# Last decode round of a hybrid-mixer kernel: where two branch granules and one row scaling stand in each engine's order

## The reference

```
u = rms_norm(x) @ w_in                      # HGRN2 q/f/i/gate, differential-attention q/k/v, merge gates
o_hg = hgrn2_recurrence(...)                # chunkwise, per head, with a state
o_hg = rms_norm(o_hg) * silu(hgate)
y_hg = o_hg @ w_branch_hg
p    = softmax(q k^T * s + bias)            # two maps per head, over prompt or over pages
o_da = rms_norm((p[0] - lam * p[1]) @ v) * 0.8
y_da = o_da @ w_branch_da
mixed = (sigmoid(g_hg) * y_hg + sigmoid(g_da) * y_da) @ w_out
x = x + rms_norm(mixed);  x = x + rms_norm(ffn(rms_norm(x)))
```

## Time and profile before

| | before |
|---|---|
| median of three runs | 1906.81 us |
| profiled execution, its time | 1907.26 us |
| profiled execution, span of the trace | 1905.7 us |
| PE busy | 1894.5 us (99% of the span) |
| DVE busy / ACT busy | 1044.4 us (55%) / 829.0 us (44%) |
| granted PE clock | 0.999 of full speed |
| last round and the first eight branch granules | about 780 to 838 us of the span |

### The profile page before, as it was taken

How to read it: one execution, slowest core, us unless ns; L and a number is a source line. 1 busy time by engine, 2 the same in 40 slices (tenths; PEclk the granted TensorE clock), 3 DMA queues, 4 the chain that set the end, 5 groups by cost and what they waited for, 6 DMA issues and landing times.

```text
span 1905.7 us, 38358 instructions
## 1 busy us (share of the span) xinstructions
PE 1894.5 (99%) x14806; PEld 1784.0 (94%) x14806; DVE 1044.4 (55%) x1342; ACT 829.0 (44%) x1099; POOL 74.5 (4%) x119
## 2 busy tenths in 40 slices
PE   9999999999999999999999999999999999999998
PEld 9999888888888888799999999999999999999998
DVE  7443655646555465665547844445444455545555
ACT  6333454535444354554445433333333334445454
POOL 1001010000000000000000000000000000000000
PEclk9999999999999999999999999999999999999999
DMA  8877898989999899988444544544444544544541
GB/s 310 179 259 256 320 351 335 376 323 354 349 339 364 321 364 352 320 309 287 153 157 146 174 158 145 172 167 163 161 153 157 167 165 156 164 160 147 177 155 56
DMA packets 123982, 444.13 MB, mean 233 GB/s; under 512 B 14581, under 2 KB 18709, under 8 KB 123856
## 3 DMA queue, kind: packets, MB, share of 16 engines
q1 hardware_dynamic: 112720, 402.31, 58.8%
q0 software_dynamic: 9968, 39.48, 7.0%
q10 hardware_dynamic: 1232, 1.47, 0.2%
HBM read 423.28 MB, written 22.54 MB: 234 GB/s over the span
## 4 chain that ended last, share of the span: by engine, by line
PE 97%; DVE 1%; DMA 1%; ACT 1%; issue 0%; SPq 0%; ACTq 0%; DVEq 0%
PE ps L426 23%; PE ps L428 22%; PE ps L427 22%; PE ps L1838 5%; PE ps L1839 5%; PE ps L1840 5%; PE ps L928 3%; PE ps L963 3%; PE ps L1480 3%; PE ps L437 1%; PE ps L937 1%; DMA raw<-w_hg 0%; PE ps L749 0%; PE ps L736 0%; DVE ffn L1800 0%
## 5 line engine op out<-in xcount | busy, mean ns | idle before, releaser
L369 DVE TENSOR_TENSOR w_lo<-raw,w_hi 128x1024 fp32r<-128x1024 f32 x416 | 503.7, 1223 | 483.2 <-ACT w_hi L364 244.4
L426 PE MATMUL ps<-x_hi,w_hi 128*128 128x320 f32 x1472 | 450.5, 306 | 0.0
L427 PE MATMUL ps<-x_hi,w_lo 128*128 128x320 f32 x1472 | 440.8, 299 | 0.0
L364 ACT ACTIVATE w_hi<-raw 128x1024 fp32r<-128x1024 f32 x236 | 246.5, 1058 | 371.8 <-PE ps L428 349.2
L428 PE MATMUL ps<-x_lo,w_hi 128*128 128x320 f32 x1344 | 401.9, 299 | 0.0
L426 PE MATMUL ps<-h_hi,w_hi 128*128 128x320 f32 x1280 | 382.7, 299 | 0.0
L427 PE MATMUL ps<-h_hi,w_lo 128*128 128x320 f32 x1280 | 382.7, 299 | 0.0
L428 PE MATMUL ps<-h_lo,w_hi 128*128 128x320 f32 x1280 | 382.7, 299 | 0.0
L426 PEld LDWEIGHTS ps<-x_hi,w_hi 128*128 128x128 f32 x1472 | 278.7, 189 | 36.3 <-issue 28.8
L427 PEld LDWEIGHTS ps<-x_hi,w_lo 128*128 128x128 f32 x1472 | 278.9, 189 | 0.1
L428 PEld LDWEIGHTS ps<-x_lo,w_hi 128*128 128x128 f32 x1344 | 254.0, 189 | 0.0
(11 more groups left out here) (330 smaller groups left out, 2355.6 us busy)
## 6 DMA issues: line engine op xcount, KB each, us to landing
raw<-w_in SPq DMA_DIRECT2D x176, 512.0 KB, 6.3
raw<-w_up SPq DMA_DIRECT2D x176, 512.0 KB, 3.5
raw<-ck SPq DMA_DIRECT2D x128, 512.0 KB, 6.4
raw<-cv SPq DMA_DIRECT2D x128, 512.0 KB, 6.8
raw<-w_dn SPq DMA_DIRECT2D x88, 512.0 KB, 3.5
raw<-w_out SPq DMA_DIRECT2D x32, 512.0 KB, 4.3
uT<-stage POOLq DMA_DIRECT2D x14, 640.0 KB, 3.9
raw<-w_hg SPq DMA_DIRECT2D x16, 512.0 KB, 4.8
```

Of the source, the lines that this page charges most:

```text
L364: act.activation(w_hi[slot % HALVES][:, :], raw[slot][:, :], ACT.Copy).then_inc(hi_ready, 1)
L369: dve.tensor_tensor(w_lo[half][:, :], raw[slot][:, :], w_hi[half][:, :].bitcast(F32), ALU.subtract).then_inc(lo_ready, 1)
L426: pe.matmul(out, wh[:, c, m, :], paired(xh(c)), start=first, stop=False)
L427: pe.matmul(out, wl[:, c, m, :], paired(xh(c)), start=False, stop=False)
```

## The change

Three lists are edited, only in the last round. On PE, granule 1 goes ahead of `turn` (it stood behind it), granule 2 goes between `turn` and `turn_new` (it stood behind the second `values`), granule 3 stays where it was, now alone between the second and third `values`. On ACT, the scaling of the output rows ("o") goes ahead of hi-5. On DVE, "o" (L900) goes ahead of lo-5. No operation is added or removed, and SyncE's and POOL's lists are the same.

```diff
@@ act_last
-            for k in (4, 5):
-                branch_hi(act, 0, k)
+            branch_hi(act, 0, 4)
             act_pages(act, r, "o")
+            branch_hi(act, 0, 5)
             act_pages(act, r, "ot")
@@ vec_last
-            for k in (4, 5):
-                branch_lo(dve, 0, k)
+            branch_lo(dve, 0, 4)
             vec_pages(dve, r, "o")
+            branch_lo(dve, 0, 5)
@@ pe_last
             pe_branch(pe, 0, 0)
+            pe_branch(pe, 0, 1)
             turn(pe, r)
-            pe_branch(pe, 0, 1)
+            pe_branch(pe, 0, 2)
             turn_new(pe, r)
             norm_sums(pe, r)
             values(pe, r, 0)
             values(pe, r, 1)
-            pe_branch(pe, 0, 2)
             pe_branch(pe, 0, 3)
```

## The result

| | before | after |
|---|---|---|
| median of five runs | 1906.49 us (1906.16 to 1907.19) | 1916.05 us (1915.38 to 1917.50) |
| ratio | | 1.005, 95% interval 1.0039 to 1.0061 |
| profiled execution, time and span | 1907.26 / 1905.7 us | 1915.80 / 1914.2 us |

The change costs 9.6 us. The forecast was 1916.0 us, so the sum was right; two of its terms were off in opposite directions, the gate's load by +0.9 us and the clock by -0.5 us, and they cancelled in part.

The account below looks back on a forecast made before the run. PE bounds the kernel, busy 1894.5 of 1905.7 us. Waits to the third value burst +5.9, rows scaled early -0.6, three clock falls +3.9: +9.2 us on 1906.8 gives 1916.0 us; 8-in-10 range 1911.5 to 1919.5.

Parts of the forecast that it names:

- the gate's load: Before granule 8: load lands 8.8 us after issue, as before; PE waits 2.1 us for the gate's product L1224.
- the clock: Behind the new waits of 3.6, 3.3 and 2.1 us: one fall each at 1.3 us, 3.9 us in all.
- The turn's wait goes: Granule 1 ahead of the turn covers PE's wait for the exponential (L937): 1.0 us saved.
- Granule 2 waits 3.6 us for lo-2: Behind the turn: hi-2 and lo-2 stay behind turn-dependent work on ACT and DVE, a new PE wait of 3.6 us.
- what I had left open about the landing: At hi-2 on ACT: the trace agreed with p0 holding hi-2, but did not exclude a late landing.
- hi-2 would otherwise be done during granule 0: On ACT: if it could reorder past p0, hi-2 would finish during granule 0 and the wait would be none.
- Granule 3 waits 3.3 us for "hl": Between second and third value bursts: granule 2 no longer covers the chain from turn_new to hl, new wait 3.3 us.
- nothing shortens this chain: Chain from turn_new to hl, 7.59 us: each step waits for the one before, so it stays whole.
- Rows scaled early: Turn back: wait 1.63 to 0.6 us, no fall; of 2.7 us 0.6 arrives, granule 8 at S (PE's sum end) + 16.9.
- less backlog might make the load quicker: Rival note on the gate's load: with PE late, weight loads ahead in the queues have got ahead; shared chance 0.25.
- The cover of the loads: Value pages and granules 4 and 5: loads move with PE, more idle DMA time ahead, costed at nothing.
- my rival of 1914.7 us: No third fall at granule 8: 5.3 + 2.6 = 7.9 us; quicker gate or two falls, chance 0.25.

Follow-up runs that it names:

- halves of granule 2: Changed kernel with hi-2 ahead of p0 on ACT and lo-2 ahead of p1 on DVE: 1911.35 us, +4.5 us, ratio 1.0025.
- one load in the changed kernel: Changed kernel with only the first merge gate's load issued at the use of value page 8: 1913.59 us, +7.0 us, ratio 1.0036.
- all four gate loads early: Kernel before plus the ACT and DVE edits, all merge gates' loads issued at the use of value page 8: 1910.77 us, +3.9 us, ratio 1.0019.
- halves of granule 3: Changed kernel with hi-2, lo-2 ahead of the copies, plus hi-3 and square-root table load ahead of pn, lo-3 ahead of the norm: 1907.67 us, ratio 1.0005.
- all remedies: Changed kernel with halves of granules 2 and 3, the table load and the first gate's load all early: 1908.64 us, +2.0 us, ratio 1.0012.
- only the first gate load early: Kernel before plus the ACT and DVE edits, first gate load at value page 8's use, other three behind the sequence's output: 1906.51 us, ratio 1.0001.

## Why the prediction was right, and where it was right by luck

- **The turn's wait goes.** Right: L937 has no wait.
- **Granule 2 waits 3.6 us for lo-2.** Right: 3.39 in the trace, 3.58 from start to start (801.35 + 1.71 to 806.64). The kernel with halves of granule 2 early shows the cause; it takes the wait down to 0.66 us. It also settles what I had left open about the landing: hi-2 started at 801.77 there, with the turn not yet over, so in the changed kernel, where hi-2 started at 804.21, ACT's order did hold it. But my sentence that hi-2 would otherwise be done during granule 0, with no wait, was wrong. In the kernel before SyncE issued that load only at 796.68, with granule 0 already running (795.66 to 799.03):

```profile
796.68 0.46 SPq L799 DMA_DIRECT2D raw<-w_hg  x1
```

and the load took 5.8 us to hi-2's start in the one kernel and 6.6 in the other. So of the 3.39 us about 2.7 are the order and 0.7 the landing. The Trainium skill's page "TensorE: Matmul & The Clock Gate" has ScalarE as strict FIFO in the table at its head; the trace agrees (hi-2 at 804.21, behind p0 at 803.29, in the changed kernel).
- **Granule 3 waits 3.3 us for "hl".** Right: 3.25. Granule 2's move alone has it too. But "nothing shortens this chain" was wrong: lo-3 and the table load were in it without need, and moving them took 1.25 us off.
- **Rows scaled early: L976 at 0.6 us, no fall at granule 4, and little of it arriving, for the gate's product.** The path was right, the size off. The term "landed 8.8 us after issue, as before" measured 10.0 us; granule 8 started at S + 17.8, not S + 16.9. So this part gave back nothing (+0.3 us against before) where I had a gain of 0.6. My own note that less backlog might make the load quicker had the sign wrong; why it took longer no run shows (in the eight other profiled executions with this load behind the sequence's output it took 8.9 to 9.6 us). And the gap at L976 was not made by ACT's order alone, as I had read it. Nor had hi-4 "long been done": in the kernel before its weight landed just in time to end at 820.36, at S itself:

```profile
819.30 1.06 ACT L364 ACTIVATE w_hi<-raw 128x1024 fp32r<-128x1024 f32 x1 [7.65 <-DMA raw<-w_hg]
```

Where PE was later, the gap was smaller with the old lists as well (1.00 us with PE's order alone, 0.59 with either granule alone), so the fall at granule 4 that I credited to the edit of ACT goes without it.
- **The cover of the loads.** I had put it at nothing. In the profiled execution of the change it holds (hi-4 starts at 824.55, 4 us ahead of S), but in the one of PE's order alone, without the fall at granule 3, the load landed at 825.5 and hi-5 delayed the scaling by 0.4 us.
- **The clock, three falls at 1.3 us.** Wrong in count and in price: two falls at 1.7 us in the profiled execution, none behind the wait of 2.86 us. 3 x 1.3 = 3.9 and 2 x 1.7 = 3.4 are 0.5 apart. Two falls and none at granule 8 was the condition of my rival of 1914.7 us; that the median came out at the forecast and not there is luck: the two falls cost 0.8 us more than I had put on two, and the gate's load 0.9 us more.
- **The sum.** By the trace, 5.8 (waits up to the third burst) + 3.4 (two falls) + 0.3 (S to granule 8) = 9.5 us; the forecast was 5.9 + 3.9 - 0.6 = 9.2. The gate's load was 0.9 dearer and the clock 0.5 cheaper. Behind granule 8 nothing was absorbed: the two profiled executions are 8.6 us apart at granule 8 and 8.5 at the end.

In the trace the difference at granule 8 is 846.50 - 837.91 = 8.6 us, since in the changed kernel's execution everything was already 0.9 us ahead when the exponential ended:

```profile
798.82 0.19 ACT L820 ACTIVATION_READ_ACCUMULATOR s_all<-s_all,mxk 128x1 f32 x1
```

against 799.76 in the earlier trace rows. The edit lies behind that point, so this is scatter of the execution, and the stretch itself lost 9.5 us. The medians are 9.6 apart.

## What to carry to other kernels

Where each engine works through its own list, filling a wait on one engine means moving everything that feeds the filler on the others too: granule 2 was put into a gap of PE while its halves stayed behind the very step whose result PE had just produced. Before a filler is moved, read from the old trace when its inputs were finished, relative to the step that it is moved behind, and what it used to cover where it stood. When the halves are moved as well, look at when their weight lands: it is the next limit (0.66 and 1.40 us here). And look for the operation that had a few tenths to spare in front of a later step (here the gate's product, 0.15 us): it is the one that takes the gain.

## What the runs showed of the hardware

The length of a wait alone did not decide whether TensorE's clock fell from 2.4 to 1.2 GHz (from 1.00 to 0.50 in the windows). The profiled executions have the same waits with and without a fall behind them:

| wait | fall | no fall |
|---|---|---|
| 3.39 us | the change, PE's order alone, one load in the changed kernel | |
| 3.25 us | the change, one load in the changed kernel, halves of granule 2 | PE's order alone, granule 2's move alone |
| 2.5 to 3.2 us | all four gate loads early (3.14) | the change (2.86), halves of granule 2 (2.50) |
| 1.9 to 2.0 us | each granule's move alone (1.93, 1.98), halves of granule 3 (2.00), all remedies (1.99) | halves of granule 3, before granule 8 (2.00) |
| 1.3 to 1.6 us | the kernel before (1.63) | PE's order alone (1.57), all remedies (1.40), ACT and DVE edits alone (1.31, 1.28) |
| 1.1 and 0.9 us close together | granule 1's move alone | |
| 0.8 to 0.9 and 0.46 us close together | only the first gate load early (0.94) | all four gate loads early (0.91), ACT and DVE edits alone, first time (0.84) |

Where a whole granule shows the price, a fall cost 1.4 to 1.7 us, and 2.9 us once. The number of falls is probably a good part of the spread: in PE's order alone the mean clock goes from 0.999 in the run of 1913.13 us to 0.996 in that of 1917.78, while the ACT and DVE edits alone, whose traces show no fall in this round, cover 1.8 us the first time and 1.3 the second. It is not all of it, or not shown to be: the kernel before covers 3.8 to 4.5 us in its 21 to 33 runs. Differences of a microsecond in such kernels can't be read from one execution, and hardly from five.
